# Recurrent mixer of a two-block transformer: level mask converted in the network ahead, first head's two gates in own buffers, last two heads woven at a higher pace

## What is computed

```python
def hgrn2_mixer(h_lat, h_ctx, w_in, lb, out_norm, w_o, with_ctx_out):
    def gates(z):
        f = lb + (1.0 - lb) * jax.nn.sigmoid(z.astype(jnp.float32))
        return heads(jnp.log(f)), heads(1.0 - f)
    def recurrent_inputs(h):
        z_fw, z_bw, v = jnp.split(h @ w_in[:, 2 * HGRN_WIDTH:], 3, axis=-1)
        g_fw, k_fw = gates(z_fw)
        g_bw, k_bw = gates(z_bw)
        return g_fw, k_fw, g_bw, k_bw, heads(v)
    def readout(o, g):
        o = rms_norm_2(o.transpose(0, 2, 1, 3), out_norm...)
        o = o * jax.nn.sigmoid(g)...
        return o.reshape(b, t, HGRN_WIDTH) @ w_o
    ...
    o_fw, _ = hgrn2_chunk_scan(q, k_fw, g_fw, v, s_fw)
    o_bw, _ = hgrn2_chunk_scan(flip(q), flip(k_bw), flip(g_bw), flip(v), s_bw)
    return readout(o_fw + flip(o_bw), gate), y_c
```

## Time and profile before

| | us |
|---|---|
| median of three runs | 2903.56 |
| lowest and highest run | 2891.17, 2906.2 |
| profiled execution, its device time | 2908.61 |
| profiled execution, its span | 2906.8 |
| mean granted clock of TensorE | 0.97 of full |
| PE busy in the span | 2636.3 (91%) |
| DVE busy in the span | 1562.5 (54%) |

### The profile page before, as it was taken

How to read it: one execution, slowest core, us unless ns; L and a number is a source line. 1 busy time by engine, 2 the same in 40 slices (tenths; PEclk the granted TensorE clock), 3 DMA queues, 4 the chain that set the end, 5 groups by cost and what they waited for, 6 DMA issues and landing times. The chain is left out here.

```text
span 2906.8 us, 39454 instructions
## 1 busy us (share of the span) xinstructions
PE 2636.3 (91%) x15228; PEld 2204.6 (76%) x15228; DVE 1562.5 (54%) x2393; ACT 1100.1 (38%) x2031; POOL 1101.1 (38%) x617
## 2 busy tenths in 40 slices
PE   1799889999999799999899999996999998799998
PEld 1566667778888677776788888885787887688887
DVE  2545426764454636556765555555567677622224
ACT  2354443332222545555422112124555555532222
POOL 2236424444444422212332333233444444244444
PEclk9999999999999999999899999997999999799999
DMA  5454214433333100001133333321111111022222
GB/s 201 155 190 160 93 48 145 149 119 135 124 130 138 44 23 23 23 23 37 64 138 138 109 111 129 117 80 43 52 44 52 51 51 60 21 101 95 95 99 76
DMA packets 81562, 267.84 MB, mean 92 GB/s; under 512 B 8672, under 2 KB 16480, under 8 KB 81376
## 3 DMA queue, kind: packets, MB, share of 16 engines
q1 hardware_dynamic: 78000, 257.59, 25.3%
q10 hardware_dynamic: 3088, 6.42, 0.6%
q0 software_dynamic: 288, 1.31, 0.1%
HBM read 260.57 MB, written 4.72 MB: 91 GB/s over the span
## 5 line engine op out<-in xcount | busy, mean ns | idle before, releaser
L2121 POOL TENSOR_TENSOR SLO<-RAW,SHI 128x1024 fp32r<-128x1024 f32 (+1 forms) x335 | 817.1, 2442 | 1277.0 <-ACT SHI L1952 1271.4
L1952 ACT ACTIVATE SHI<-RAW 128x1024 fp32r<-128x1024 f32 (+1 forms) x335 | 345.4, 1035 | 1078.2 <-PE PS L2379 1056.6
L2377 PE MATMUL PS<-HLh,SHI 128*128 128x512 f32 (+1 forms) x1800 | 706.1, 392 | 20.1 <-ACT HLh L1966 7.6
L2378 PE MATMUL PS<-HLl,SHI 128*128 128x512 f32 (+1 forms) x1800 | 681.9, 379 | 0.0
L2379 PE MATMUL PS<-HLh,SLO 128*128 128x512 f32 (+1 forms) x1800 | 681.8, 379 | 0.0
L2377 PEld LDWEIGHTS PS<-HLh,SHI 128*128 128x128 f32 x1800 | 343.7, 191 | 94.1 <-issue 31.4
L2379 PEld LDWEIGHTS PS<-HLh,SLO 128*128 128x128 f32 x1800 | 342.7, 190 | 63.6
L2378 PEld LDWEIGHTS PS<-HLl,SHI 128*128 128x128 f32 x1800 | 343.8, 191 | 60.5 <-issue 5.6
L2377 PE MATMUL PS<-hh,SHI 128*128 128x512 f32 (+1 forms) x1016 | 366.5, 361 | 7.6 <-POOL hl L2140 3.0
L2379 PE MATMUL PS<-hh,SLO 128*128 128x512 f32 (+1 forms) x1016 | 357.6, 352 | 0.0
L2378 PE MATMUL PS<-hl,SHI 128*128 128x512 f32 (+1 forms) x1016 | 356.0, 350 | 0.0
(11 more groups left out here) (233 smaller groups left out, 3966.6 us busy)
## 6 DMA issues: line engine op xcount, KB each, us to landing
RAW<-in_k_w SPq DMA_DIRECT2D x317, 512.0 KB, 3.5
ADA<-in_k_w SPq DMA_DIRECT2D x132, 512.0 KB, 4.3
early<-in_k_w SPq DMA_DIRECT2D x12, 512.0 KB, 9.6
RAW<-in_k_w SPq DMA_DIRECT2D x18, 256.0 KB, 2.6
XL<-in_xT ACTq DMA_DIRECT2D x1, 2048.0 KB, 12.6
bi<-in_k_bias SPq DMA_DIRECT2D x16, 128.0 KB, 3.6
out<-XL SPq DMA_DIRECT2D x16, 128.0 KB, 1.8
bi<-in_k_bias SPq DMA_DIRECT2D x8, 192.0 KB, 4.4
```

What stands on the lines that cost most here:

```text
L1952: eng.activation(u.hi, u.w, ACT.Copy).then_inc(S["a_hi"], 1)
L2121: eng.tensor_tensor(u.lo, u.w, u.hi.bitcast(F32), ALU.subtract).then_inc(S["g_lo"], 1)
L2377: eng.matmul(st.out, lh, rh, start=st.first and j == 0, stop=False)
L2378: eng.matmul(st.out, lh, rl, start=False, stop=False)
```

## The change

Four edits. (1) The mask is loaded when attention of the second block ends, into a free place, and converted 20 steps into the feed-forward network of the first layer, to the unused tail of the ROPE buffer. (2) Head 0's backward gate takes the buffers `ek` and `kt` (one column longer) in place of the ring `t`; a new DVE step `Zero` clears one column. (3) Head 0's `hhead` waits, before its `DiagQ`, until `hg(0)` has been put, so that values and output gate come ahead of it. (4) When head 6 begins, the heads' pace goes from 0.36 to 0.75; the output projection of head 6 alone (`hwo6`) is added to the dense work, and `turnover` keeps head 7's alone.

```diff
@@ the loader, and the network ahead
+    HMASK = ROPE[:, TT:TT + 224].bitcast(U8)
+    mstage = place("hmstage", [128, 896], F32, AR + 60000)[:, :]
+    d_hm, t_hm = dma("act", mstage, t_in["k_hmask"], hfree), []
...
+    def with_mask(main):
+        for i, _ in enumerate(main):
+            if i == 20:
+                t_hm.append(tick("v_hmask"))
+                put(HMask(HMASK, mstage, d_hm, t_hm[0]))
+            yield
@@ the mixer's start
-    c = W["xy"].cells[3]
-    t_hm = tick("v_hmask")
-    put(HMask(W["hm"].cells[0].ap, c.ap[:, 0:896], dma("act", c.ap[:, 0:896], t_in["k_hmask"], blk), t_hm))
-    c.free = [t_hm]
+    HM = HMASK.rearrange("p (l n) -> p l n", l=7)
+    t_zero = tick("v_zero")
+    put(Zero(W["kt"].cells[0].ap[:, 0:1], blk, t_zero))
@@ hgate
-        a, g = W["t"].next(), W["t"].next()
+        a, g = (W["ek"].cells[0], W["kt"].cells[0]) if (h, d) == (0, 1) else (W["t"].next(), W["t"].next())
@@ hhead
+        if h == 6:
+            heads_pace[0] = 0.75
...
+        if h == 0:
+            yield from after("g 0 of the mixer")
         At = W["A"].next()
@@ dense work, and what follows
+    def hwo6():
+        yield from after("head 6")
+        yield from accum(lambda c0: ([getunit("hwo", ktiles(6, 1), seg(0, 1024))], 1024), heads_out[6:7],
+                         [lat_part(gates(2, 2, 0))])
-    dense += [hwo(4)]
-    weave((pipelined([hhead(h) for h in range(8)]), 0.36), (pipelined(dense), 1.0))
+    dense += [hwo(4), hwo6()]
+    weave((pipelined([hhead(h) for h in range(8)]), heads_pace), (pipelined(dense), 1.0))
-    turnover([getunit("hwo", ktiles(6, 2), seg(c0, 512)) for c0 in (0, 512)], 512, heads_out[6:8],
+    turnover([getunit("hwo", ktiles(7, 1), seg(0, 1024))], 1024, heads_out[7:8],
```

More of the change, by code:

```diff
@@ L197 @@
 Up = namedtuple("Up", "f src hi lo t_mm t_silu t_mul t_free t_hi t_lo")
+Zero = namedtuple("Zero", "ap t_free t_done")
 HMask = namedtuple("HMask", "dst src t_in t_done")
@@ L429, in weave @@
                     left.remove(p)
-                now = p[2] = (max(now, p[2]) if p[3] else p[2]) + (work[0] - before + 1) / p[1]
+                now = p[2] = (max(now, p[2]) if p[3] else p[2]) + (work[0] - before + 1) / (p[1][0] if type(p[1]) is list else p[1])
                 p[3] = False
@@ L1539, in build_program @@
     hid = hids(W)
-    main_with(bg, ffn(W, hid, 1, cat, [lat_part(gates(1, 5, 0)), ctx_part(gates(1, 5, 1))]), 6)
+    def with_mask(main):
[4 more added lines that the diff above has]
+            yield
+    main_with(bg, with_mask(ffn(W, hid, 1, cat, [lat_part(gates(1, 5, 0)), ctx_part(gates(1, 5, 1))])), 6)
     put(Table("natural_log_exp_and_others"))
@@ L1548, in build_program @@
     W = arena({"v": (1, 6 * 256, F32, 4), "xy": (4, 2 * TT, F32, 4), "kk": (2, TT, F32, 4), "q": (2, NT, F32, 4),
-               "sg": (2, NT, F32, 4), "t": (2, TT + 1, F32, 4), "ek": (1, TT, F32, 4), "eq": (1, NT, F32, 4),
-               "R": (1, 2 * NT, F32, 4), "A": (1, NT, F32, 4), "kt": (1, TT, F32, 4), "S": (4, 128, F32, 4),
+               "sg": (2, NT, F32, 4), "t": (2, TT + 1, F32, 4), "ek": (1, TT + 1, F32, 4), "eq": (1, NT, F32, 4),
+               "R": (1, 2 * NT, F32, 4), "A": (1, NT, F32, 4), "kt": (1, TT + 1, F32, 4), "S": (4, 128, F32, 4),
                "f": (1, NT, F32, 4), "r": (1, NT, F32, 4), "hh": (2, NT, F32R, 4), "hl": (2, NT, F32R, 4),
-               "hm": (1, 7 * 128, U8, 1), "pe": (4, 8, F32, 4), "de": (4, 8, F32, 4)}, blk)
+               "pe": (4, 8, F32, 4), "de": (4, 8, F32, 4)}, blk)
     hid = hids(W)
@@ L1556, in build_program @@
     W["R"] = Ring([W["R"].cells[0].ap, *(t[:, :] for t in ADA)], blk)
-    HM = W["hm"].cells[0].ap.rearrange("p (l n) -> p l n", l=7)
-    c = W["xy"].cells[3]
-    t_hm = tick("v_hmask")
-    put(HMask(W["hm"].cells[0].ap, c.ap[:, 0:896], dma("act", c.ap[:, 0:896], t_in["k_hmask"], blk), t_hm))
-    c.free = [t_hm]
+    HM = HMASK.rearrange("p (l n) -> p l n", l=7)
+    t_zero = tick("v_zero")
+    put(Zero(W["kt"].cells[0].ap[:, 0:1], blk, t_zero))
     H = {}
@@ L1589, in tail @@
             put(GateF(a.ap[:, 0:TT], kc.ap, lnf, LB[:, 4, h:h + 1], LB[:, 0, h:h + 1], [t_s, t_lb], t_f, kc.free, t_kk,
-                      g.free, t_g, t_k))
+                      g.free + [t_zero], t_g, t_k))
             yield
@@ L1768, in hlevels @@
                 yield
+    heads_pace = [0.36]
     def hhead(h):
+        if h == 6:
+            heads_pace[0] = 0.75
         yield from after(f"gate {h} 0")
@@ L2269, in up, with zero @@
                 eng.tensor_tensor(st.lo, st.f, st.hi.bitcast(F32), ALU.subtract).then_inc(S["v_ulo"], 1)
+            def zero(st):
+                v.wait_ge(st.t_free)
+                eng.memset(st.ap, 0.0).then_inc(S["v_zero"], 1)
             def hmask(st):
@@ L2356, in _ @@
             own = {Setup: setup, Square: square_, NormA: norm_a, NormB: norm_b, Ada: ada_, Coef: coef_, VCopy: vcopy, HNorm: hnorm, HRope: hrope, Score: score, Flip: flip_,
-                   Share: share, OutNorm: onorm, GMul: gmul, GSum: gsum, Resid: resid, Up: up, HMask: hmask, LowerB: lowerb,
+                   Share: share, OutNorm: onorm, GMul: gmul, GSum: gsum, Resid: resid, Up: up, HMask: hmask, Zero: zero, LowerB: lowerb,
                    ZMax: zmax, GateF: gate_f, GateX: gate_x, ScanS: scan_s, LevA: lev_a, LevB: lev_b, LevC: lev_c,
```

## The result

The changed kernel takes **2881.9 us** (median of 4 runs, 2880.6 to 2883.5) against 2901.1 (median of 4, 2891.2 to 2906.2) of the kernel before: ratio 0.9934, 95% interval 0.9907 to 0.9960, or 19.3 us less. The forecast was 2872, 31.5 us less. The direction was right and most of the first end's gain came; the last end gained nothing, and the whole is 0.61 of what was forecast.

What follows compares the result with a forecast made beforehand. PE, busy 91%, was taken as the bound, so time could be won only where it idles, at the mixer's two ends. 26 + 5 + 1 less 0.5 for the mask gave 31.5 us off 2903.56, 2872 us; range 2856 to 2891.

Steps and rivals of the forecast that it cites:

- the forecast's own case: Whole kernel: the gains at both ends and turnover come as forecast, 2862 to 2884 us by its bounds; chance 0.62.
- three signs of being wrong: Head 0's window over 62 us, PE waiting during the values, or the last end losing.
- Rival (d): First end: PE stops at the values for a bank or split, so the gap stays; 11 us won, near 2892; chance 0.06.
- 26 us: First end: `DiagQ` of head 1 at 2072 against 2098.53, 26 us won, bounds 34 and 14.
- Serially 34.8 + 14.4 = 49; ... I take 47: Head 0's recurrence: head 7's 34.8 us alone plus head 1's two gates, 14.4, part of it filling DVE idle; 47 us.
- 6.6 us of slack covers them: Head 0's start: key sum ends at 2015.4, PE arrives at 2022.0, so edits 1 and 2 are worth 0.4 us at `DiagQ`.
- +5: Last end, `DiagQ` of head 6 to `turnover`: 93.6 of 98.75 us, 5 won; bounds 11 won and 6 lost.
- I take 13.5 left: Last end: of DVE's 24.6 us of waits 13.5 remain, beside 80.1 us of DVE work, giving 93.6 us.
- All waits kept: Last end, lower bound: all of DVE's 24.6 us of waits stay, 6 us lost.
- rival (b): The recurrence takes a gap back: head 0 still takes 62.0 us, last end even or slightly losing; 10 won, 2893; chance 0.16.
- (a): PE-bound all through: head 0 at PE's 42 us, last heads at DVE's 88; 47 us won, 2857; chance 0.12.
- (c): Recurrence sets both windows: first end loses 1.5 us, last end loses too; in all 23 us slower, 2927; chance 0.04.

Runs made afterwards that it cites:

- v_key_no_pace: Changed kernel with head 0 waiting for the values and not its output gate, and edit 4 undone; median 9 us below the changed kernel's, first stretch 71.6 us.
- v_key: Changed kernel with head 0 waiting for the values and no longer for its output gate; four executions 2870.8 to 2877.8 us, first stretch 73.1 us against 80.4.
- short_splits: Kernel before with edits 3 and 4, three of POOL's splits writing 8 columns, not 128 (values not right); head 0's window 54.18 us, 59.85 with full splits.
- no_pace: Changed kernel with edit 4 undone (pace 0.36 throughout, no separate projection of head 6); 2881.5 us against 2881.9, last stretch 1.8 us shorter.

## Why the forecast was right, and where it was off

The measured time lies within the range, and inside the forecast's own case of 2862 to 2884, but near its slow end. The mechanism was right at the first end; at the last end a gain of 6 us was forecast and none came, so a part of the agreement is owed to the width of the range. (That case's bounds are narrower than the bounds of its terms: all at their best are 48 us won, 2856, and all at their worst 6, 2898.) One of the three signs of being wrong came: the last end lost.

**The gap.** Right nearly to the number. Value products ran from 1996.69 on with no pause over 0.7 us, banks and splits allowed it, the output gate ended at 2020.5, and `DiagQ` of head 0 had no wait. The mixer began 1.64 us earlier than before; with this taken off, the key sum's end, forecast for 2015.4, came at 2014.81 + 1.64 = 2016.5, and `DiagQ`, forecast for 2022.0, at 2022.1. Rival (d) fell with it.

**Head 0's window: the term that was mis-sized.** I had 26 us, from 100.2 to 73.9 between the first value product and `DiagQ` of head 1; measured are 19.8, since the window is 56.6 us and not 50. The step that was mis-sized is "Serially 34.8 + 14.4 = 49; ... I take 47". From the first subtraction (2021.28) the last product of head 0 ended 53.8 us later (2075.05), not 47. Seen from PE: 47.9 busy and 8.7 idle, where I had 42 of work and so 8 idle. 42 is 1.8 too little even at full clock (the forecast's own terms, 69.88 - 21.4 - 6, give 42.5): `v_key_no_pace` needs 47.81 for 287 products, of which 17 are the output gate's, at 0.235 us 4.0, so 43.8 for the 270. The other 4.1 of the 5.9 us I put down to slow clock, as what is left. Its places show in the granted clock, two slices of the window:

```profile
2030.00:2040.00 10.00, 10.00 (x59) 8.85 (x58) 2.66 (x5) 8.82 (x17) 4.91 (x3) 0.88 0.01 2
...
2070.00:2077.10 7.10, 6.24 (x25) 5.79 (x26) 3.38 (x5) 0.60 (x1) 1.96 (x2) 0.53 0.23 77
```

The first follows the wait of 3.3 us for level 0, the second the one of 4.6 us for `eq`; by the missing share of the clock they lost about 1.2 and 2.9 us. I took the slow clock off with the gap and did not ask whether the recurrence's own waits bring it back. In this trace they do, and so its wait of 4.6 us cost more than 4.6.

**The recurrence bounds the window.** Right, and my price for it was the wrong part. I wrote that head 0 starts 1.5 us later with PE 25 us ahead, and that the output gate's clip stands before it on DVE; I didn't ask what it would be worth to take it away. `v_key` shows 7.3 us for the key.

**Edits 1 and 2 at 0.4 us.** Wrong by a factor of ten, 3.8 us. The step was "6.6 us of slack covers them": it asked only whether the key sum is in time for `DiagQ`. It is; but on ACT and POOL the same chain stands ahead of the splits, and when it ends later, the splits slide onto DVE's first subtractions. `short_splits` shows that step: with the old chain and without those splits the first stretch is 78.5 us. Alone they are worth 9.3 us, not the 6.95 I had without the cover. I had looked at this kind of contention at the last end only.

**Middle and mask.** 306.3 us, and 310 forecast. The 3.5 us less were not forecast; they are in the kernels without the change of the start or of the end as well, as said above, and without them the span would have fallen by 21.6 us and not 25.1. The mask's move could not be seen by itself.

**Last end and turnover.** Wrong. I had +5 from `DiagQ` of head 6 to `turnover`, from 98.75 to 93.6; measured are 57.84 + 44.67 = 102.5, so -3.8, and for what follows +3.5 (42.32 from 2507.11 on before, 38.81 now), where I had +1. Together -0.3, against `no_pace` -1.8. The step that failed is "I take 13.5 left", the waits of DVE, for which the forecast had no sum: busy 40.93 + 33.62 = 74.6 us, even below my 80.1, and waits 28.0 us, more than the 24.6 of before. DVE's idle time before its steps, in head 6's window of the changed kernel:

```profile
DVE sg L2322 <- PE PS L2404: 9.1, 1, 9.1
DVE t L2326 <- ACT t L2054: 5.5, 2, 2.8
DVE f L2367 <- ACT r L2115: 2.1, 1, 2.1
```

The quicker head puts its output gate's clip where PE has not yet got to that gate's last product, and DVE stands for 9.1 us. That is such a "PE-side wait" as I said could go; in the kernel before it was 6.7 us. All DVE's waits in head 6's window are 16.9 us, 12.4 before. Dense work in head 7's window did not fill DVE's waits there either: 11.1 us, 12.3 before. Its 7 waits for PE before updates of XL, 4.6 us in all, and 3.4 us before a level's copy took the place of others. All waits kept was the bound I gave, 6 lost; 3.8 is within it. A sum of an engine's work is no forecast of a stretch in which the engines hand each other every step.

**The contention there** went the way that was counted: in the group of the earlier trace rows, level subtractions at head 6 fell from 1.561 us each to 1.024, those at head 7 rose from 0.822 to 0.962:

```profile
L2354 DVE TENSOR_TENSOR ADA<-xy 128x512 f32<-128x512 f32 x10 | 9.6, 1024 | 0.0
...
L2354 DVE TENSOR_TENSOR ADA<-xy 128x512 f32<-128x512 f32 x8 | 7.4, 962 | 0.0
```

With the group that writes R, all level subtractions are 23.3 us at head 6 before and 16.9 now, 10.0 and 12.1 at head 7. The 9.8 us that whole splits could have cost head 7 did not come: three splits are in its window now, 8.1 us, and its 13 subtractions take 12.1 us where 12 took 10.0. But the DVE time regained at head 6 brought no time there, since DVE spent it waiting.

**The sum.** 26 + 5 + 1 - 0.5 was forecast; measured are 19.8 at the first end and nothing at the last, and 19.3 us in the medians; that these two agree so closely is partly chance, as the spans of the two traces differ by 25.1. It lies between the forecast's case and rival (b): head 0 ran faster than the 62 us of (b), and the last end was even, as (b) has it. (a) failed on both its parts, (c) on head 0.

## What to carry to other kernels

When a dense block is to fill a gap ahead of a serial chain, let the chain's first steps pass as soon as the block has enough work in hand: the last dense group, with its in-order clip on the chain's engine, set ahead of the chain, cost 7.3 us of the stretch here (5.6 in the medians). "In time for its reader" is not the whole price of a late chain: look at what else stands behind it on each engine, and beside which instructions that will fall. And where a stretch is a weave of two engines' steps, try the order before counting its gain; the three ways tried here to move the same products lost 2, 6 and 11 us of the last stretch against leaving them.

## What was not expected of the hardware

- Four 128x512 subtractions with both inputs in SBUF took 3.32, 5.28, 7.46 and 9.29 us beside no full split of POOL's, one, two, and three (2.65, 5.46 and 8.46 us). I had seen 0.82 and 1.56 us as averages and had not expected a factor of 2.8 in one place. One by one they took 0.68 us alone and up to 3.27 (in `v_key_no_pace`) beside a split.
- A wait of 3.3 us for level 0 in the changed kernel was followed by products of 512 columns at 0.43 us (2030.27, 2030.70) up to 2031.98, a clock of 1.2 GHz; in `v_key_no_pace` a wait of 3.5 us at the same place left the granted clock at 1.00 throughout the window. A wait of about the same length brought the lower clock in one trace and not in the other.
- The start of the mixer differs by 7.5 us between two traces with the same code ahead of it, more than most effects studied here.
